# Feed-forward layers of a two-block network: 20 of 22 gate and up tiles as seven block products in place of eight

## The reference

```python
def _rmsnorm(x, g):
    xf = x.astype(jnp.float32)
    y = xf * lax.rsqrt(jnp.mean(xf * xf, axis=-1, keepdims=True) + EPS)
    return (y * g.astype(jnp.float32)).astype(x.dtype)

def _swiglu(x, w_gate, w_up, w_down):
    return (jax.nn.silu(x @ w_gate) * (x @ w_up)) @ w_down

x = x + MACARON * _swiglu(_rmsnorm(x, ffn1_norm), ffn1_w_gate, ffn1_w_up, ffn1_w_down)
```

## Time and profile before

| what | value |
|---|---|
| median of 3 runs | 3212.49 us (3212.03 to 3212.8) |
| profiled execution, its span | 3210.8 us |
| PE busy | 3203.0 us, 14706 matmuls |
| DVE busy | 1548.0 us, 1849 instructions |
| ACT busy | 1086.8 us, 1449 instructions |
| POOL busy | 1327.6 us, 550 instructions |
| granted TensorE clock | 1.000 of full speed |

### The profile page before, as it was taken

One profiled execution on the slowest core, in us unless ns is written; L12 is line 12 of the kernel. 1 busy time (PEld: TensorE's weight loads), 2 busy tenths in 40 slices (PEclk: granted clock), 3 DMA queues, 4 the chain that ended last, 5 costly groups with the idle time before them and its releaser, 6 DMA issues.

```text
span 3210.8 us, 36140 instructions
## 1 busy us (share of the span) xinstructions
PE 3203.0 (100%) x14706; PEld 2655.4 (83%) x14706; DVE 1548.0 (48%) x1849; ACT 1086.8 (34%) x1449; POOL 1327.6 (41%) x550
## 2 busy tenths in 40 slices
PE   9999999999999999999999999999999999999999
PEld 7888888888888888888888877888888888888888
DVE  6442266554234431476444268545444486454421
ACT  4222333322232223333222355543223475432222
POOL 4444433544444444434444433235444212254443
PEclk9999999999999999999999999999999999999999
DMA  4223322322232322322323332323323333232222
GB/s 153 98 98 100 120 82 79 108 97 97 98 108 97 99 99 99 123 79 87 104 92 100 108 93 73 124 92 105 99 92 102 99 98 126 99 106 98 98 92 86
DMA packets 93236, 321.54 MB, mean 100 GB/s; under 512 B 10512, under 2 KB 14992, under 8 KB 93072
## 3 DMA queue, kind: packets, MB, share of 16 engines
q1 hardware_dynamic: 87680, 312.07, 29.4%
q10 hardware_dynamic: 5392, 7.17, 0.7%
HBM read 316.05 MB, written 2.10 MB: 99 GB/s over the span
## 4 chain that ended last, share of the span: by engine, by line
PE 99%; DVE 0%; ACT 0%; DMA 0%; issue 0%; ACTq 0%; DVEq 0%
PE bank L383 20%; PE bank L387 20%; PE bank L384 20%; PE bank L398 9%; PE bank L399 9%; PE bank L405 9%; PE bank L368 1%; PE bank L369 1%; PE bank L372 1%; PE bank L696 0%; PE bank L824 0%; PE bank L823 0%; PE bank L565 0%; PE bank L829 0%; PE bank L558 0%; PE bank L559 0%
## 5 line engine op out<-in xcount | busy, mean ns | idle before, releaser
L2600 POOL TENSOR_TENSOR wlo<-raw,whi 128x1024 fp32r<-128x1024 f32 x535 | 1324.3, 2485 | 1862.9 <-ACT whi L1017 1862.5
L1017 ACT ACTIVATE whi<-raw 128x1024 fp32r<-128x1024 f32 x588 | 611.3, 1052 | 585.3 <-PE bank L405 413.2
L383 PE MATMUL bank<-gxh,whi 128*128 128x512 f32 x1536 | 600.4, 391 | 0.0
L384 PE MATMUL bank<-gxl,whi 128*128 128x512 f32 x1536 | 597.7, 389 | 0.0
L398 PE MATMUL bank<-gxh,whi 128*128 128x512 f32 x1248 | 487.3, 390 | 1.3 <-ACT whi L1017 1.2
L399 PE MATMUL bank<-gxl,whi 128*128 128x512 f32 x1248 | 485.7, 389 | 0.0
L383 PE MATMUL bank<-f_hh,whi 128*128 128x512 f32 x1034 | 402.2, 389 | 0.0
L384 PE MATMUL bank<-f_hl,whi 128*128 128x512 f32 x1034 | 402.2, 389 | 0.0
L387 PE MATMUL bank<-gxh,wlo 128*128 128x512 f32 x1536 | 379.6, 389 | 0.0
L1832 DVE TENSOR_TENSOR f_u<-bank,R 128x512 f32<-128x512 f32 x132 | 91.2, 691 | 582.9 <-PE bank L405 582.9
L383 PEld LDWEIGHTS bank<-gxh,whi 128*128 128x128 f32 x1536 | 288.4, 188 | 60.9 <-issue 0.7
(11 more groups left out here) (415 smaller groups left out, 3584.7 us busy)
## 6 DMA issues: line engine op xcount, KB each, us to landing
raw<-stream SPq DMA_DIRECT2D x588, 512.0 KB, 3.3
xa_mem<-memT ACTq DMA_DIRECT2D x2, 1024.0 KB, 6.2
m_dk<-decay ACTq DMA_DIRECT2D x2, 514.0 KB, 4.5
x<-xT ACTq DMA_DIRECT2D x4, 256.0 KB, 5.3
x<-xT SPq DMA_DIRECT2D x4, 256.0 KB, 6.7
outT<-x SPq DMA_DIRECT2D x2, 512.0 KB, 3.0
m_ct<-cos ACTq DMA_DIRECT2D x2, 256.0 KB, 2.7
m_sn<-sin ACTq DMA_DIRECT2D x2, 256.0 KB, 3.1
```

The lines of the kernel that those rows point to most:

```text
L383: pe.matmul(out, seq(hi, k, P), h, start=first and k == 0, stop=False)
L384: pe.matmul(out, seq(hi, k, P), l, start=False, stop=False)
L1017: act.activation(M.whi[r][:, :], M.raw[r][:, :], ACT.Copy).then_inc(*S.tick("hi", u))
L2600: pool.tensor_tensor(M.wlo[r][:, :], M.raw[r][:, :], M.whi[r][:, :].bitcast(F32), ALU.subtract).then_inc(*S.tick("lo", u))
```

## The change

**Products.** In tiles m = 2 to 21 of every feed-forward stage the gate and up units are seen as a 2 x 2 block matrix (features k = 0 to 3 and 4 to 7 by gate and up), and gx as a 2 x 2 block matrix (the same features by tokens 0 to 255 and 256 to 511). Their eight block products are replaced by seven (Strassen's scheme in Winograd's form), each of 4 blocks x 3 matmuls with 256 columns. Tiles 0 and 1 stay as they were.

**Sums of weights.** For each such tile DVE forms four sums of weight blocks (`sums`: s1 and s3 as one 128 x 1024 instruction, s2 and s4 into PSUM banks 5 and 6), ACT rounds them (`s13_hi`, `s24_hi`, `m22_hi`), DVE takes their low parts (`s13_lo`, `s24_lo`), and POOL only those of the up unit and of one 128 x 512 block.

**Sums of x.** Once a stage, for k = 0 to 3, ACT, DVE, ACT and DVE again make four sums of quarters of gx with high and low parts (`take_gain`, `turn_parts`, `turn_hi`, `turn_lo`). Two of the four k are done in the stage before from its output tiles 5, 6 and 7 on, the other two after the stage's R; in stage 0 all four after R.

**Sums of results.** ACT copies three partial results out of PSUM (`snap`), DVE adds two into PSUM (`c22`, `first_row`).

**Gate and up.** R is no longer applied to the up result but to the down result (`scaled_part`), a DVE instruction more for each. The rounding to `f_hh` moves from DVE to ACT (`hidden_hi`).

**Three parts.** The down projection is done in three parts, over inner tiles 0 to 5, 6 to 13 and 14 to 21, behind tiles 6, 14 and 21; each of 8 units, added to x by DVE. The down units are laid out anew (24, as before). DVE's work for the first Strassen tile of the next run (`begin`) is put after the part's output tile 4.

The core of the diff, PE and the two helpers of ACT:

```diff
 F_SCALE = (0.5, 0.5, 0.5, 0.5, 1.0, 1.0)
+F_PARTS = ((0, 6), (6, 14), (14, 22))
+F_RUNS = ((0, 7), (7, 15), (15, 22))
...
+        def product(n, m, weights, lo_event, moving, out, first, arrive=None):
+            hi, lo = weights
+            for k in range(4):
+                if arrive:
+                    pe.wait_ge(*S.at(*arrive[k]))
+                pe.matmul(out, seq(hi, k, P), moving[k][0], start=first and k == 0, stop=False, skip_group_check=n != 1)
+                pe.matmul(out, seq(hi, k, P), moving[k][1], start=False, stop=False, skip_group_check=n != 1)
+            pe.wait_ge(*S.at(*lo_event))
+            for k in range(4):
+                mm = pe.matmul(out, seq(lo, k, P), moving[k][0], start=False, stop=k == 3, skip_group_check=n != 1)
+            mm.then_inc(*S.tick("seven", f, m, n))
...
+        def fourth(m):
+            x, g = bank[BANK["a", f, m]], U["gate", f, m]
+            pe.wait_ge(*S.at("hi", g))
+            pe.wait_ge(*S.at("c22", f, m))
+            product(4, m, (seq(T[f"sh{m % 2}"], 0), seq(T[f"sl{m % 2}"], 0)), low_part(g), turns[3], x[:, 0:HALF], False)
...
+        def quad(m, before):
+            g, u, x = U["gate", f, m] % SLOTS, U["up", f, m] % SLOTS, next_bank("a", f, m)
+            sh, sl = T[f"sh{m % 2}"], T[f"sl{m % 2}"]
+            up_lo = low_part(U["up", f, m])
+            pe.wait_ge(*S.at("hi", U["up", f, m]))
+            product(1, m, (seq(M.whi[u], 0), seq(M.wlo[u], 0)), up_lo, gx_part[1, 1], x[:, 0:HALF], True)
+            y = next_bank("t", f, m)
+            pe.wait_ge(*S.at("s13_hi", f, m))
+            product(5, m, (seq(M.whi[g], 0), seq(M.wlo[g], 0)), ("s13_lo", f, m), turns[0], y[:, HALF:], True,
+                    [("turned_lo", f, k) for k in range(4)] if m == PLAIN else None)
+            if before is not None:
+                fourth(before)
+            pe.wait_ge(*S.at("s24_hi", f, m))
+            pe.wait_ge(*S.at("snap1", f, m))
+            product(6, m, (seq(sh, 1), seq(sl, 1)), ("s24_lo", f, m), turns[2], x[:, 0:HALF], False)
+            pe.wait_ge(*S.at("snap5", f, m))
+            product(2, m, (seq(M.whi[u], 1), seq(M.wlo[u], 1)), up_lo, gx_part[2, 1], y[:, 0:HALF], False)
+            product(3, m, (seq(sh, 2), seq(sl, 2)), ("s24_lo", f, m), gx_part[2, 2], y[:, HALF:], False)
+            pe.wait_ge(*S.at("snap6", f, m))
+            product(7, m, (seq(M.whi[g], 1), seq(M.wlo[g], 1)), ("s13_lo", f, m), turns[1], x[:, 0:HALF], False)
...
-            project(("gate", f, m), next_bank("a", f, m)[:, :], i if m == 0 else None)
-            b = next_bank("u", f, m)
-            high(("up", f, m), b[:, :])
...
+        for m in range(0 if f else 1, PLAIN):
+            plain(m)
+        for c in range(2):
+            run(c)
+            pairs, arrive = hidden(c)
+            for m in range(KD):
+                unit(("down", f, c, m), next_bank("part_scaled", f, c, m)[:, :], pairs, arrive=arrive if m == 0 else None)
+                if m == 0:
+                    fourth(F_RUNS[c][1] - 1)
+        run(2)
+        pairs, arrive = hidden(2)
+        banks = []
+        for m in range(X_EARLY):
+            banks.append(next_bank("part_scaled", f, 2, m))
+            part(("down", f, 2, m), banks[m][:, :], pairs, range(0, 6), True, False, arrive if m == 0 else None)
             if m == 0:
-                norm(i)
-            low(("up", f, m), b[:, :])
-        residual(i, [("down", f, m, j) for m in range(KD) for j in range(3)],
-                 [(seq(T["hh"], k), seq(T["hl"], k)) for k in range(KF)], [("hidden", f, k) for k in range(KF)])
+                fourth(KF - 1)
+        for m in range(X_EARLY):
+            part(("down", f, 2, m), banks[m][:, :], pairs, range(6, KD), False, True, arrive if m == 0 else None)
+        for m in range(X_EARLY, KD - 1 if f == 5 else KD):
+            unit(("down", f, 2, m), next_bank("part_scaled", f, 2, m)[:, :], pairs)
         if f == 5:
-            last_tile([(seq(T["hh"], k), seq(T["hl"], k)) for k in range(KF)])
+            last_tile(pairs)
...
+    def take_gain(f, k):
+        if k:
+            act.wait_ge(*S.at("turned_parts", f, k - 1))
+        act.activation(M.f[f]["gained"][:, :], seq(M.x, k), ACT.Copy, scale=gain_after(M, F_STAGE[f] - 1)(k)).then_inc(
+            *S.tick("gained", f, k))
+    def turn_hi(f, k):
+        T = M.f[f]
+        act.wait_ge(*S.at("turned_parts", f, k))
+        for n in range(2):
+            act.activation(T["th"][:, k * 2 * SEQ + n * SEQ:k * 2 * SEQ + (n + 1) * SEQ], seq(T["parts"], n), ACT.Copy,
+                           scale=-1.0 if n else 1.0).then_inc(*S.tick("turned_hi", f, k))
```

ACT's list:

```diff
+        def run(c):
+            first, end = max(F_RUNS[c][0], PLAIN), F_RUNS[c][1]
+            for m in range(first, end):
+                x, y, more = bank[BANK["a", f, m]], bank[BANK["u", f, m]], m + 1 < end
+                split_hi(U["up", f, m + 1] if more else U["down", f, c, 0])
+                snap(1, m, x[:, 0:HALF], T["c16"][:, 0:HALF], "c1")
+                if more:
+                    s13_hi(m + 1)
+                else:
+                    split_hi(U["down", f, c, 1])
+                snap(5, m, y[:, HALF:], T["c5"][:, :], "c22")
+                if more:
+                    s24_hi(m + 1)
+                    m22_hi(m + 1)
+                if m > first or c == 0:
+                    silu(m - 1)
+                snap(6, m, x[:, 0:HALF], T["c16"][:, HALF:], "c1")
+                if m > first or c == 0:
+                    hidden_hi(m - 1)
+        def begin(m):
+            split_hi(U["up", f, m])
+            s13_hi(m)
+            s24_hi(m)
+            m22_hi(m)
+        ahead(("gate", f, 0))
+        if not f:
+            root(i)
+        ahead(("up", f, 0))
+        if f:
+            root(i)
+        else:
+            take_gain(0, 0)
+            turn_hi(0, 0)
+            take_gain(0, 1)
+            turn_hi(0, 1)
+            take_gain(0, 2)
+        turn_hi(f, 2)
+        take_gain(f, 3)
+        turn_hi(f, 3)
```

DVE's list:

```diff
+        def c22(m):
+            x = at_bank("a", f, m)
+            dve.wait_ge(*S.at("seven", f, m, 7))
+            dve.wait_ge(*S.at("snap5", f, m))
...
+        def gate(m):
+            if m < PLAIN:
+                dve.wait_ge(*used("gate", f, m))
+            else:
+                dve.wait_ge(*S.at("seven", f, m, 4))
+                dve.wait_ge(*S.at("c22", f, m))
             if m:
                 dve.wait_ge(*S.at("silu", f, m - 1))
-            dve.tensor_tensor(T["a"][:, :], at_bank("a", f, m)[:, :], M.R[:, :], ALU.mult).then_inc(*S.tick("a", f, m))
-            dve.wait_ge(*used("up", f, m))
+            dve.scalar_tensor_tensor(T["a"][:, :], at_bank("a", f, m)[:, :], 1.0 if m < PLAIN else -1.0, M.R[:, :],
...
+        def gated(m):
+            if m < PLAIN:
+                dve.wait_ge(*used("up", f, m))
+            else:
+                dve.wait_ge(*S.at("c1", f, m))
+            dve.wait_ge(*S.at("silu", f, m))
             if m:
                 dve.wait_ge(*S.at("hidden", f, m - 1))
-            dve.tensor_tensor(T["u"][:, :], at_bank("u", f, m)[:, :], M.R[:, :], ALU.mult).then_inc(*S.tick("u", f, m))
-            dve.wait_ge(*S.at("silu", f, m))
-            dve.wait_ge(*S.at("u", f, m))
...
+        def hidden_lo(m):
             dve.wait_ge(*S.at("t", f, m))
-            dve.tensor_scalar(seq(T["hh"], m), T["u"][:, :], 1.0, None, ALU.mult).then_inc(*S.tick("hh", f, m))
             dve.wait_ge(*S.at("hh", f, m))
-            dve.tensor_tensor(seq(T["hl"], m), T["u"][:, :], seq(T["hh"], m).bitcast(F32), ALU.subtract).then_inc(
-                *S.tick("hidden", f, m))
...
+        def run(c):
+            first, end = max(F_RUNS[c][0], PLAIN), F_RUNS[c][1]
+            for m in range(first, end):
+                before, more = m > first or c == 0, m + 1 < end
+                if m > first:
+                    c22(m - 1)
+                if more:
+                    sums(m + 1)
+                    s13_lo(m + 1)
+                if before:
+                    gate(m - 1)
+                if more:
+                    s24_lo(m + 1)
+                if before:
+                    gated(m - 1)
+                if before:
+                    hidden_lo(m - 1)
+                first_row(m)
+            m = end - 1
+            c22(m)
+            gate(m)
+            gated(m)
+            hidden_lo(m)
+        rstd(i)
+        dve.wait_ge(*S.at("rstd", i))
+        for k in range(2 if f else 0, 4):
+            turn_parts(f, k)
+            turn_lo(f, k)
+        gate(0)
+        gated(0)
+        hidden_lo(0)
+        begin(PLAIN)
+        for c in range(2):
+            run(c)
+            for m in range(KD):
+                dve.wait_ge(*used("down", f, c, m))
+                scaled_part(f, c, m, at_bank("part", f, c, m)[:, :], M.R)
+                dve.scalar_tensor_tensor(seq(M.x, m), T["u"][:, :], F_SCALE[f], seq(M.x, m), ALU.mult, ALU.add).then_inc(
+                    *S.tick("part_sum", f, c, m))
```

(4 more changed lines are left out.)

305 lines of the change are left out of this document (239 added, 66 removed).

## The result

The changed kernel takes **3330.99 us** (median of 4 runs, 3330.51 to 3332.58) against 3212.64 us (3212.03 to 3213.14) on the same chip: a ratio of 1.037, 95% interval 1.0355 to 1.0384. It is slower, as forecast, but by 118.4 us where 41.5 were forecast, and the time lies above the range.

A forecast was written before the change was run, and what follows sets the result against it. PE's issue was taken to bound the kernel: -96.6 us of matmul time, +3 mid-run, +25.6, +2.8, +34.8, +45 and +26.4 for entries and hand-overs, +0.5 tail, make +41.5 on 3212.5: 3254 us, range 3180 to 3292.

The forecast's parts named there:

- What bounds the kernel, and the gain: PE's issue sets the time; gate and up tiles fall from 10.88 to 10.08 us, 96.6 us won in all.
- The collisions: DVE instructions with two SBUF inputs wait for a POOL instruction under way, about 2.4 us; 75 us charged in all.
- The middle of a run: Tiles within runs: DVE needs 9.4 of 10.08 us, so PE hardly waits; 3 us lost over 102 tiles.
- (a): Stage entry, gx: turns between outputs 5 and 7 end 4.7 us late; four stages 18.8, with stage 3 25.6 us.
- (b): Entry, wait for tile 2 behind the chain from R: 4.0 us in five stages, 14.8 in stage 0; 34.8 together.
- (c): Entry, first Strassen tile, nothing prepared: PE waits 7.5 us in each of six stages, 45 us.
- (d): Start of runs 2 and 3: `snap5` late behind a held addition to x, 2.2 us twelve times, 26.4 us.
- The other four stages behind a feed-forward wait 0.7 each for the extra instruction: 2.8: Hand-over from feed-forward stages: `scaled_part`, one more DVE instruction, costs 0.7 us in each of four following stages.
- A: Rival: collisions do not fall where placed, 55% of their 75 us falls away; faster, 3179 us; chance 0.20.
- B: Rival: DVE sets the pace mid-run, some 0.3 us a tile lost 102 times; 3285 us; chance 0.10.
- D: Rival: half-width matmuls do not keep 0.120 us between changing banks and waits, gain gone; 3350 us; chance 0.04.
- C: Rival: PE's clock falls in waits at six entries, 0.107 us more a matmul, 12 to 54 us; 3280; chance 0.12.

The follow-up runs named there:

- poolset: Changed kernel with POOL writing zeros where it subtracted, so that it reads nothing from SBUF: 3198.06 us, ratio 0.996.
- psum: Changed kernel with the down result scaled by R in its own PSUM bank and x added from there: 3295.92 us, ratio 1.026.
- best6: Changed kernel with scaled outputs and turned sums in PSUM, `snap5` and `snap6` first, three plain tiles with mixed lists, angles and small mixer instructions spread, earlier scaling: 3191.73 us.
- inter3: Changed kernel with three plain tiles in place of two, tile 2's units split earlier and gates of tiles 0 and 1 between the turns' rounds: 3295.93 us.
- turns_in: Changed kernel with all four rounds of turns (sums of x) behind R in every stage, none in the stage before: 3338.35 us, ratio 1.0395.
- ang: Changed kernel with the angles of the mixer behind stage 5 moved from the last part to behind output 1 of the second part: 3325.96 us.
- best7: best6 with the angles moved as in ang and no longer spread over three outputs: 3184.98 us, ratio 0.992.
- best5: best6 with `s13` in two PSUM banks and ACT waiting for s2 in place of s13: 3223.15 us, ratio 1.004.
- turnsp: Changed kernel with the sums for the turned inputs and the right half of `f_gained` in PSUM banks: 3302.08 us, ratio 1.028.

## Why the prediction was wrong, point by point

- **What bounds the kernel, and the gain**: right. 0.227 and 0.120 us a matmul gave 10.08 us a tile, as measured, and 96.6 us. The 3 us for PE's waits in the middle of the runs did not come.
- **The collisions**: right, and the places named were hit. poolset shows it by taking them away, psum for the additions to x. The rule was too narrow: `f_hh`, which the prediction moved to ACT by it, has one SBUF input and is held as a fast form (last section).
- **The middle of a run**: right: PE does not wait; DVE's round fully held by POOL is 10.10 us, as best6 shows, 0.02 over PE's.
- **(a)**: the pause was right (4.58 for 4.7); the 1.5 to 2.3 us of lower clock behind it were not in the sum. +6.7.
- **(b)**: right to 0.2 us in each of six stages. inter3 removes the wait in five stages (8.84 us stay in stage 0), though half of the loss comes back inside the first Strassen tile, turns_in lengthens it there by the 8.8 us of two rounds.
- **(c)**: the sum was about right (with b 84 for 79.8), the picture was not: less waiting, more slow PE, the same chain.
- **(d)**: right in its links and in its pauses (25.9 for 26.4); the clock behind tile 7's pauses added 9 us.
- **"The other four stages behind a feed-forward wait 0.7 each for the extra instruction: 2.8"**, with stage 3's 6.8 and the tail's 0.5: **this is the step that failed**, 10.1 us for 68. It counted one instruction more and did not ask what DVE's whole round is held against: the split of the down projection in three had cut PE's cover per output from 14.96 to 5.44 us, and everything that used to sleep behind it (rounds of 5.47 us, 6.4 us of angles, the turns at stage 3) came out at once. psum took 30 us of the 68 away by shortening the rounds, ang 6.5 by moving the angles, and turns_in 6.9 by taking the turns out of stage 3's hand-over; taken together in best7 such changes removed 37 of the 68, and the 31 that stay there are put down to the same cause without a run that shows it. The section on the middle of a run made this very comparison for a tile; it was not made for an output.
- **The rivals**: A, B and D did not happen in the changed kernel (B did in best5, by another edit). C, the clock, did, at more places than it counted, and gave 18 us on the path, inside its 12 to 54. Its price of 0.107 us a matmul was high: 0.213 against 0.120 us are 0.093. Even forecast and C together, 3280, would have been 51 us low: the hand-overs were in no case, and so the range was too narrow upwards.

What stays open: the extra 3 us of the tail was measured, not taken apart (PE waits 2.14 us for ACT's `sq` there, which it did not before), and (c)'s first wait for POOL (1.07 us) was not tried alone.

## What to carry to other kernels

When a sum is split in parts, the cover of every piece of side work that was hung on its pieces shrinks by the same factor: redo the comparison "side engine's round against PE's round" for each loop, the hand-overs first, not only for the loop that the change is about. Price a pause by the distance of two fixed points on both sides of it, not by its own length: a slower clock behind it added 1.5 us to a pause of 2.42, and elsewhere was hidden wholly. Putting one operand of a DVE instruction on a tight chain into PSUM while POOL works on SBUF gave 35 and 29 us in psum and turnsp; where it made ACT wait, in best5, it cost 31. And put in an engine's list first what another engine waits for.

## What the runs showed of the hardware that was not expected

- A DVE instruction with one tensor input, in SBUF, is held by POOL too, if it is one of the fast ones (copies, casts and instructions of a tensor with a scalar, 0.43 us for 512 columns). In psum, beside a subtraction of POOL of 2.60 us, where the form takes 0.43 us elsewhere:

```profile
1893.33 2.62 DVE L2008 TENSOR_SCALAR m_rsin<-m_rsin,rcol 128x512 f32<-128x512 f32 x1
```

- The same pause, 2.42 us, with the same work on either side, was followed by 3.4 us at 1.2 GHz in stage 0 of turns_in and by full clock in its other stages. None of the six pauses of 1.90 us in the changed kernel was followed by the lower clock, one of turnsp's was (1.5 us more). What tells them apart is not in the rows.
- POOL's instruction is 0.95 us for 128 x 1024 when it only writes, and 2.4 when it reads two operands. Only the latter holds DVE's instructions with two SBUF inputs; the former still holds the fast forms (in poolset all four of 512 columns that began beside it took 0.93 to 1.03 us in place of some 0.43).
- At 1.2 GHz matmuls start 0.213 us apart with 256 columns and 0.427 with 512, exactly twice as far for twice the columns; at 2.4 GHz 0.120 and 0.227, each 0.013 us more than half of that.
